# One inference step of a hybrid retention and mixture-of-experts layer: sums in two f32r products, the last w_down run in two landings, the last expert's product split by contraction

## The reference

```
def expert_block(args):                      # 1024 -> 2048 -> 1024, per expert
    gu = xb @ w_gu[e] + b_gu[e]
    gate, up = gu[:, :D_FF], gu[:, D_FF:]
    gate = jnp.minimum(gate, 7.0); up = jnp.clip(up, -7.0, 7.0)
    h = (up + 1.0) * gate * jax.nn.sigmoid(1.702 * gate)
    return h @ w_down[e] + b_down[e]
f = sum over the token's four experts of gate_weight * expert_output
y = layer_norm(2 ** 0.25 * h + f, ln2_g, ln2_b)
```

## Time and profile before

| | before |
|---|---|
| median of 3 runs | 1126.11 us |
| lowest and highest | 1124.74 and 1128.12 us |
| profiled execution, its time | 1127.85 us |
| its span | 1125.9 us |
| PE busy in the span | 1078.4 us (96%) |
| mean DMA rate over the span | 387 GB/s |

### The profile page before, as it was taken

The page is one execution under the profiler, slowest core; times in us unless marked ns, Lnnn a source line. Parts: engine busy times, 40 slices in busy tenths (PEclk is TensorE's granted clock), DMA queues, the critical chain, the costliest instruction groups (busy, mean ns, idle before and its releaser), DMA issues.

```text
span 1125.9 us, 13553 instructions
## 1 busy us (share of the span) xinstructions
PE 1078.4 (96%) x5542; PEld 547.0 (49%) x5542; DVE 330.0 (29%) x589; ACT 193.4 (17%) x335; POOL 102.8 (9%) x56
## 2 busy tenths in 40 slices
PE   8999999999999999999999999999898989898994
PEld 5889968535434343434343434343434343343431
DVE  3487976212130303030312121203030302121114
ACT  3244311111111111111120202011111111111101
POOL 4676440000000000000000000000000000000002
PEclk9999998999999999999999999999999999999998
DMA  9960299999999999999999999999999999999993
GB/s 351 335 221 1 90 394 383 368 416 400 423 427 427 428 427 428 428 428 427 428 428 428 428 428 428 428 428 428 428 428 428 428 428 428 429 428 428 427 427 132
DMA packets 53667, 436.26 MB, mean 387 GB/s; under 512 B 5952, under 2 KB 15936, under 8 KB 26912
## 3 DMA queue, kind: packets, MB, share of 16 engines
q1 hardware_dynamic: 47104, 428.67, 91.6%
q10 hardware_dynamic: 6528, 7.09, 1.8%
HBM read 431.78 MB, written 3.97 MB: 387 GB/s over the span
## 4 chain that ended last, share of the span: by engine, by line
PE 65%; DMA 24%; DVE 2%; ACT 0%; POOL 0%; issue 0%; DVEq 0%; SPq 0%; ACTq 0%; POOLq 0%
PE bank L955 25%; DMA ring<-w_down 21%; PE bank L981 17%; PE bank L891 8%; PE bank L606 4%; DMA old_rooms<-w_down 3%; PE bank L1007 1%; PE bank L936 1%; PE bank L1009 1%; PE bank L806 1%; PE bank L796 1%; PE bank L964 1%; PE bank L739 1%; DVE mixed_lo L1469 0%; PE bank L900 0%; PE bank L776 0%
## 5 line engine op out<-in xcount | busy, mean ns | idle before, releaser
L955 PE MATMUL bank<-ring,xg 128*64 128x512 f32 x1536 | 345.2, 595 | 7.1 <-DMA ring<-w_gu 7.1
L955 PEld LDWEIGHTS bank<-ring,xg 128*64 128x64 f32 x1536 | 105.4, 136 | 209.2 <-issue 187.8
L981 PE MATMUL bank<-ring,act_t 128*64 128x512 f32 x672 | 150.7, 594 | 7.0 <-DMA ring<-w_down 7.0
L955 PE MATMUL bank<-old_rooms,xg 128*64 128x512 f32 x496 | 112.4, 595 | 4.7 <-DMA old_rooms<-w_gu 4.7
L1642 DVE SCALAR_TENSOR_TENSOR oo_lo<-oo_raw,gate_s,oo_hi 128x512 fp32r<-128x512 f32 x32 | 24.0, 751 | 311.2 <-ACT oo_hi L1202 311.2
L1669 DVE TENSOR_SCALAR gate_c<-bank 128x512 f32<-128x512 f32 x32 | 22.1, 691 | 263.7 <-PE bank L955 263.7
L891 PEld LDWEIGHTS bank<-onehot,hid 128*128 128x128 f32 x720 | 85.9, 196 | 12.2 <-issue 12.2
L1279 POOL TENSOR_TENSOR rstd<-veps,minus_half 128x1 f32<-128x1 f32 x6 | 3.3, 545 | 953.9 <-DVE veps L1460 953.9
L981 PEld LDWEIGHTS bank<-ring,act_t 128*64 128x64 f32 x672 | 46.2, 136 | 90.7 <-issue 78.3
L891 PE MATMUL bank<-onehot,hid 128*128 128x128 f32 x720 | 88.8, 283 | 0.0
L1655 DVE TENSOR_TENSOR xy<-xy,bank 128x512 f32<-128x512 f32 x84 | 52.7, 682 | 107.7 <-PE bank L1009 107.7
(11 more groups left out here) (226 smaller groups left out, 947.2 us busy)
## 6 DMA issues: line engine op xcount, KB each, us to landing
ring<-w_gu SPq DMA_DIRECT2D x90, 2048.0 KB, 30.5
ring<-w_down SPq DMA_DIRECT2D x41, 2048.0 KB, 33.0
old_rooms<-w_gu SPq DMA_DIRECT2D x30, 2048.0 KB, 30.2
old_rooms<-w_down SPq DMA_DIRECT2D x13, 2048.0 KB, 32.9
ring<-w_in SPq DMA_DIRECT2D x13, 1024.0 KB, 14.5
ring<-w_gu SPq DMA_DIRECT2D x12, 1024.0 KB, 9.9
old_rooms<-w_down SPq DMA_DIRECT2D x6, 1024.0 KB, 13.9
over_q<-w_down SPq DMA_DIRECT2D x3, 2048.0 KB, 15.5
```

The costliest lines, as they stand in the source:

```text
L955: mm = pe.matmul(bank[2 * a + n][64 * hf:64 * hf + 64, :], xg[:, c, 64 * a:64 * a + 64], w[:, col:col + 512], start=False, stop=(c == KC - 1))
L981: mm = pe.matmul(bank[b][64 * hf:64 * hf + 64, :], act_t[:, a, c % 4, 64 * (c // 4):64 * (c // 4) + 64], w[:, c % run, hf * 512:(hf + 1) * ...
```

## The change

1. **Landings.** In odd pairs the last w_down run (2 MB, rooms 12 and 13) is issued as two DMAs of 1 MB: `last_low_full` tells the first landing (chunks 4 and 5), `slot_full` the second (chunks 6 and 7). TensorE waits for each where it needs it.
2. **Sums.** `sums_so_far` takes tile t as high and low float32r parts (`sums_hi` by ScalarE, the low part by VectorE into the room of `x_lo`), four products a tile, each of one pass. They are placed inside `gate_up(1)` (tiles 0, 1) and `down(0)` (tile 2).
3. **Last expert.** `down_last` gives each output half `hf` a bank of its own (5 and 4): even chunks are added up in columns 0 to 63, odd ones in 64 to 127. The two partial sums are added by the combination, whose matrix `gt_last` holds the last expert's rows twice. Since bank 4 is that of `down(0)`, TensorE waits for `out_ready` first. `oo_hi` and `oo_lo` are made from PSUM directly, without `oo_raw`.
4. **First expert of the last pair.** It is combined by itself, over 64 rows of contraction (`combine_first`, 12 products), between chunks 3 and 4 of the last product.
5. **Last norm.** The statistics of tile 2 move from VectorE to ScalarE (row sums and sums of squares by accumulated outputs). GpSimd makes all three `rstd` before tile 0's gain and bias.

The diff, cut to its core:

```diff
@@ sync: pair_pieces
-                    expert_run(j, ea, eb, rooms(g % WIDE, units)).then_inc(slot_full[g % WIDE], 16)
+                    if odd and j == PAIR_PIECES - DN_UNITS:
+                        k = (DN_PIECES - DN_UNITS) * 256
+                        rows = w_down[bass.ds(eb, 1), k:k + 128 * DN_RUN, :].rearrange("e (p k) n -> p e (k n)", p=128)
+                        for n, landed in enumerate((last_low_full, slot_full[g % WIDE])):
+                            sp.dma_start(rooms(g % WIDE, units)[:, n * PW:(n + 1) * PW].unsqueeze(1),
+                                         rows[:, :, n * PW:(n + 1) * PW]).then_inc(landed, 16)
...
@@ tensor
+            def down_last(turn, between):
+                for hf in range(2):
+                    pe.matmul(bank[last_down_banks[hf]][0:64, :], sel_down[:, 1, :],
+                              biasp[:, 2 * FF + hf * 512:2 * FF + (hf + 1) * 512], start=True, stop=False)
+                for c in range(0, KC, 2):
...
+                    for hf in range(2):
+                        for g in range(2):
+                            mm = pe.matmul(bank[last_down_banks[hf]][64 * g:64 * g + 64, :],
+                                           act_t[:, 1, (c + g) % 4, 64 * (c // 4):64 * (c // 4) + 64],
+                                           w[:, (c + g) % DN_RUN, hf * 512:(hf + 1) * 512],
+                                           start=(c == 0 and g == 1), stop=(c == KC - 2))
+                        if c == KC - 2 and hf == 0:
+                            mm.then_inc(half_down, 1)
+                    mm.then_inc(piece_used, 1)
+            def sums_so_far(t):
...
+                for hf in range(2):
+                    pe.matmul(bank[last_banks[2 * t + hf]][:, :], ident_r, sums_hi[:, t, hf * 512:(hf + 1) * 512],
                               start=True, stop=False)
+                pe.wait_ge(sums_lo_ready, t + 1)
...
+            def combine_first(p):
...
+                for hf in range(2):
+                    for t in range(NT):
+                        for part in (oo_hi, first_lo):
+                            pe.matmul(bank[last_banks[2 * t + hf]][:, :], gt[0:64, t * 128:(t + 1) * 128],
+                                      part[0:64, hf, :], start=False, stop=False)
@@ tensor: pair
                 gate_up(1, turn, odd, {4: lambda: transpose_act(0, p, 2 if first else DN_RUN)}
+                        | ({2: lambda: sums_so_far(0), 6: lambda: sums_so_far(1)} if last else {})
...
-                     | ({2: overflow_tables} if first else {}))
+                     | ({2: overflow_tables} if first else {}) | ({6: lambda: sums_so_far(2)} if last else {}))
...
-                down(1, turn, odd, {})
+                if last:
+                    pe.wait_ge(out_ready, 4 * p + 2)
+                    down_last(turn, {4: lambda: combine_first(p)})
@@ scalar
+                    act.activation(oo_hi[:, hf, :], bank[last_down_banks[hf]][:, :], ACT.Copy, scale=gate_last[:, 0:1])\
+                        .then_inc(oo_hi_ready, 1)
...
+            for n in range(2):
+                act.wait_ge(comb_mm, 6 * last_pair + NT * (n + 1))
+                act.activation((sig, gate_c)[n][:, :], bank[last_banks[2 * (NT - 1) + n]][:, :], ACT.Identity, scale=-1.0 / D,
+                               accum_out=sums[:, n:n + 1]).then_inc(row_sum, 1)
...
+            for n in range(2):
+                act.activation(act_h[:, n, :], bank[last_banks[2 * (NT - 1) + n]][:, :], ACT.Square, bias=sums[:, 2:3],
+                               accum_out=sums[:, 3 + n:4 + n]).then_inc(row_square, 1)
             act.wait_ge(y_shift, 1)
@@ gpsimd
-            row_rstd(NT)
+            for t in range(NT):
+                row_rstd(NT + t)
...
-                row_rstd(NT + 1 + n)
@@ vector: end
-            sums_stats(2)
+            last_variance()
             finish(1)
```

More of the change, by code:

```diff
@@ L977, in down @@
                         else:
-                            w = landed(j) if turn is None else run_landed(j, DN_UNITS, turn, odd)
+                            if odd and j == PAIR_PIECES - DN_UNITS:
+                                pe.wait_ge(last_low_full, 16 * turn + 16)
+                                w = run_room(j, DN_UNITS, odd)
+                            else:
+                                w = landed(j) if turn is None else run_landed(j, DN_UNITS, turn, odd)
                         w = w.rearrange("p (k n) -> p k n", n=D)
+                    if odd and a and c == KC - 2:
+                        run_landed(2 * GU_PIECES + 2 * DN_PIECES - DN_UNITS, DN_UNITS, turn, odd)
                     for hf in range(2):
@@ L1046, in pair @@
                 pe.wait_ge(act_t_ready, 2 * p + 2)
-                down(1, turn, odd, {})
+                if last:
+                    pe.wait_ge(out_ready, 4 * p + 2)
+                    down_last(turn, {4: lambda: combine_first(p)})
+                else:
+                    down(1, turn, odd, {})
                 if first:
@@ L1194, in copy_gates, with copy_last_gates @@
                     act.copy(gate_s[r, :], bank[5][r, T + a:T + a + 1]).then_inc(gt_ready, 1)
[L1196 to L1200, removed]
+            def copy_last_gates(n):
+                act.wait_ge(gt_mm, n)
+                for r in (slice(0, 64), slice(64, 128)):
+                    act.copy(gate_last[r, :], bank[5][64:128, T + 1:T + 2]).then_inc(gt_last_ready, 1)
+                    ins = act.copy(gt_last[r, :], bank[5][64:128, 0:T])
+                ins.then_inc(gt_last_ready, 1)
@@ L1217, in pair @@
                     if last and a:
[L1218 to L1220 removed]
+                        last_high_outputs(p)
+                        continue
                     act.wait_ge(piece_used, PAIR_PIECES * p + MIX_PIECES + 2 * GU_PIECES + DN_PIECES * (a + 1))
                     for hf in range(2):
[L1223 to L1225 removed]
+                        act.copy(oo_raw[64 * a:64 * a + 64, hf, :],
+                                 bank[down_banks[a]][64 * hf:64 * hf + 64, :]).then_inc(out_ready, 1)
                         if a:
[L1227 removed]
+                            high_outputs(p, hf)
+                    if last:
+                        for hf in range(2):
+                            first_high_outputs(p, hf)
                     if a == (1 if first else 0) and not last:
@@ L1629, in slots_of, with first_low_outputs, last_low_outputs, low_outputs @@
                 gates_of(n)
-            def low_outputs(p, last=False):
+            def first_low_outputs(p):
                 dve.wait_ge(gt_ready, 2 * p + 2)
                 for hf in range(2):
[L1635 to L1640, removed]
+                    dve.wait_ge(oo_hi_ready, 2 * p + hf + 1)
+                    dve.scalar_tensor_tensor(first_lo[0:64, hf, :], oo_raw[0:64, hf, :], gate_s[0:64, 0:1],
+                                             oo_hi[0:64, hf, :].bitcast(F32), ALU.mult, ALU.subtract).then_inc(oo_lo_ready, 1)
+            def last_low_outputs(p):
+                dve.wait_ge(gt_last_ready, 3)
+                for hf in range(2):
+                    dve.wait_ge(oo_hi_ready, 2 * p + hf + 3)
+                    dve.scalar_tensor_tensor(oo_lo[:, hf, :], bank[last_down_banks[hf]][:, :], gate_last[:, 0:1],
+                                             oo_hi[:, hf, :].bitcast(F32), ALU.mult, ALU.subtract).then_inc(oo_lo_ready, 1)
+            def low_outputs(p):
+                dve.wait_ge(gt_ready, 2 * p + 2)
+                for hf in range(2):
+                    dve.wait_ge(out_ready, 4 * p + 3 + hf)
                     dve.wait_ge(oo_hi_ready, 2 * p + hf + 1)
@@ L1660, in pair @@
                     add_outputs(p - 1, second)
+                if last:
+                    low_sums()
                 if first:
```

120 lines of the change are left out of this document (95 added, 25 removed).

## The result

| | before | changed |
|---|---|---|
| median (runs) | 1126.11 us (20) | 1127.99 us (20) |
| lowest and highest | 1124.74 and 1128.12 us | 1126.17 and 1130.14 us |
| profiled execution, its time | 1127.85 us | 1129.87 us |
| its span | 1125.9 us | 1128.0 us |

The ratio is 1.0019 with a 95% interval of 1.0013 to 1.0025: 2.1 us slower (1.4 to 2.8), clear of noise and under the 0.3% that were called "no change". The forecast was 1127.8 us.

A forecast was written before the change was run, and what follows sets the result against it. The weight stream was taken to bound the expert stage, so savings must follow the last bytes. Product end 3.3 us later, tail giving back 1.6 us: 1.7 us over the 1126.11 us median, 1127.8 us; range 1124.8 to 1130.4 us.

The forecast's parts named there:

- The loads cost nothing: Last run of odd pairs as two 1 MB DMAs: cost taken as nothing, below 0.1 us a pair.
- a sign against it: Weight stream in the odd pairs: a rate below 427 GB/s would show the forecast wrong.
- the estimate of 1135.3 us: Whole kernel's time if 1 MB loads ran at the Trainium skill's 341 GB/s; named beside the 6% short-loads rival.
- The sums: Tile sums in the last pair: 0.8 us saved a tile, lost for tiles 0 and 1 except 0.2 us.
- The wait for bank 4: Before the last biases: PE stands 1.35 us until ACT has copied out the first expert's bank.
- The first expert's combination: Inside the last product: twelve products and two shape changes, 2.96 us, all on the path.
- The lower bound: Products over 64 rows in the first expert's combination: half of 0.23 us each, making the twelve cost 1.4 us less.
- The product's end: End of the last product on PE: 1111.30 us, 3.34 us later than before.
- Rival 1: Last pair: savings reach the end, product ends at 1106.1 us, time 1122.6 us, faster; 10%.
- After the product: Tail of combination, norm and stores: gives back 1.6 us, so the end moves by 1.7 us.
- Rival 3: Last norm: ACT becomes the bound, each wide accumulated output costing 0.6 us more, 1129.1 us or above; 16%.

The follow-up runs named there:

- e1: Changed kernel with the last w_down run of odd pairs in one landing again; ratio to the kernel before 1.0016.
- e3: Kernel before with only the sums so far as float32r products; ratio to the kernel before 1.0009.
- e2: Changed kernel with the last expert's first run worked off half 0 first, half 1 after the wait for bank 4; ratio to the kernel before 1.0008.
- e7: Changed kernel with one of the twelve products of the first expert's own combination, output wrong; ratio to the kernel before 0.9995.
- e4: Kernel before with the sums as float32r products and the last run in two landings; ratio to the kernel before 0.9985.
- e6: Changed kernel without the norm's part: tile 2's statistics on VectorE again, powers between tile 0's operations; ratio to the kernel before 1.0014.
- e8: Kernel before with float32r sums, two landings and the norm's part in another order, tile 0 and 1 work first; ratio to the kernel before 0.9985.
- e9: e8 with the store of tile 0's second half issued last, behind both of tile 2; ratio to the kernel before 0.9982.

## Why the prediction was right

**The loads cost nothing.** Right: same GB/s, and e1 shows no price of the halves. Two slices of 426 GB/s (the 18th and the 27th) fall in odd pairs, which the forecast had named as a sign against it; but e1, without halves, has slices of 426 GB/s as well, and over 480 to 1080 us, where the halves of five of the six odd pairs land, each of the three kernels moved 428 GB/s. The figure of the Trainium skill for a load of 1 MB ("DMA: Bandwidth & Descriptors", Measured), from which the estimate of 1135.3 us came, does not carry over to this stream, where some seven loads stand in the queue at once (33 us from issue to landing at 4.9 us each): e1 and the changed kernel agree within 0.1 us in both stretches.

**The sums.** Four float32r products with their changes of shape took 1097.56 - 1096.43 = 1.13 us, taken were 1.12. That two tiles' savings are lost in waits shows in the 0.80 and 0.56 us ahead of 1089.67 and 1094.56 us, together 1.36 of 1.6 us saved, and in e3. The forecast had the wait at the second place alone; most of it came one run sooner. That the start at 1094.56 us was met exactly is in part luck, since S moves by up to 2.9 us from trace to trace.

**The wait for bank 4.** 1.35 us forecast, 1.28 us measured; the biases began at 1100.79, forecast 1100.63 us. e2 shows that it is on the path: without it S to E is 0.6 us shorter even with a landing that was 0.9 us late. Whether all 1.3 us can be had back is not shown.

**The first expert's combination.** 1107.71 - 1104.77 = 2.94 us, taken were 2.96. A product over 64 rows has the same 0.23 us spacing as one over 128. The lower bound, half of that, which the Trainium skill ("TensorEngine Tiling (Array Packing)", Theoretical Speedup) allows for products on separate tiles, was rightly not taken. e7 shows the full price.

**The product's end.** 1111.36 us, forecast 1111.30. Rival 1 needed PE 5 us earlier; no trace shows it anywhere near.

**After the product.** The mechanism was right, the size off by 0.4 us. POOL's power began at 1117.99 (forecast some 1117.8), its four operations at 1118.50 (1118.3) and they took 5.17 us where four times 1.22 were taken: with the wait for its own result between gain and bias the spacing is 1.34 us, which the power had filled before. So the tail gave back 1.3 and not 1.6 us, the span grew by 2.1 and not 1.7 us. The median, 1.9 us up, came within 0.2 us of the forecast; that it came nearer than the span is luck.

**Rival 3.** The accumulated output costs one more instruction of 0.19 us after each wide one, not 0.6 us, and even that hardly shows: from the first square to the second are 1116.27 - 1115.59 = 0.68 us, no more than an `oo_hi` takes (two in 1.47 us). The squares were through at 1117.04 us and DVE came for them at 1117.57 us.

What the experiments add: parts 1 and 2 pay together (1.2 us in the trace, e4); parts 3 and 4 give back 1.5 us after the product (e6, 16.46 us from E to the end against 17.94 us before), but part 3 brings the wait for the bank, and it needs part 4, which costs 2.9 us. Part 3 was not run by itself. The change as a whole loses time because the combination was to fill a wait that PE never had.

## What to carry to other kernels

Before work is moved to fill a wait for data, read whether the engine arrives before the data at that place: here it arrived 0.2 us before, and 3 us of fill work went straight onto the path. Two parts that each do nothing alone (less work before a landing, and a landing in two halves) can pay together, so test them as a pair and apart from the rest of the change. When a wait is taken away, look up what lands or ends next and by how much: in e2 PE came 0.3 us after the next landing's usual time, and one landing that was 0.9 us late took half of the gain.

## What the runs showed of the hardware

- Over 64 or over 128 rows of contraction, a float32r product of 512 columns starts 0.23 us after the one before it (L1068 and L1134).
- ScalarE's accumulated output is an instruction of its own of 0.19 to 0.21 us that reads it out. It overlaps the wide one before it: two squares with their readouts start 0.68 us apart.
- The last landing of the stream came 9.5 to 9.9 us after S in nine of the twelve traces, after 10.2 us in e8 and after 10.5 and 10.7 us in two others (e2: 1069.45 + 33.8 us; e3: 1068.67 + 33.9 us). In these two the run before it was late as well, by some 1 us. One trace of each doesn't tell whether it goes with the edit; a tail that hangs on it scatters by about 1 us.
- The 128x1 sum on DVE took 0.73 us in e8 and e9 and 0.15 us elsewhere. Its cause was not looked for.
